# The S5 branch of a hybrid decoder trunk: recurrence per token, or per chunk of four tokens

## The reference

```python
uf = u.reshape(bsz, s, 32, 16)                   # 32 groups of 16 channels, 64 complex states each
ab = exp(lr * dt) * (cos(li * dt), sin(li * dt))  # one decay per group and state
bb = f * (b_re, b_im)                            # f from lambda and ab
x_re, x_im = einsum('bsgc,gpc->bsgp', uf, bb)     # inputs of the states
h[t] = ab * h[t - 1] + x[t]                      # complex, over all 256 tokens
y = einsum(h_re, c_re) - einsum(h_im, c_im) + d_skip * u
z = gelu(y); g = z @ w_glu + b_glu               # then a gated linear unit
```

## Time and profile before

| | us |
|---|---|
| median of 3 runs (858.77 to 859.50) | 858.96 |
| profiled execution | 857.93 |
| its span | 856.1 |
| mean granted clock of TensorE, share of full speed | 0.987 |
| TensorE busy | 825.7 |
| VectorE busy | 561.5 |
| ScalarE busy | 312.2 |
| POOL busy | 294.9 |

### The profile page before, as it was taken

How to read it: one execution, slowest core, us unless ns; L and a number is a source line. 1 busy time by engine, 2 the same in 40 slices (tenths; PEclk the granted TensorE clock), 3 DMA queues, 4 the chain that set the end, 5 groups by cost and what they waited for, 6 DMA issues and landing times.

```text
span 856.1 us, 10220 instructions
## 1 busy us (share of the span) xinstructions
PE 825.7 (96%) x3918; PEld 611.4 (71%) x3918; DVE 561.5 (66%) x939; ACT 312.2 (36%) x519; POOL 294.9 (34%) x130
## 2 busy tenths in 40 slices
...
GB/s 250 140 245 144 192 127 122 130 141 201 94 127 168 123 148 148 120 152 152 153 70 161 244 119 198 143 125 127 146 172 147 116 132 129 137 130 170 172 147 50
DMA packets 86992, 126.56 MB, mean 148 GB/s; under 512 B 22072, under 2 KB 32672, under 8 KB 86944
## 3 DMA queue, kind: packets, MB, share of 16 engines
...
...
q10 hardware_dynamic: 176, 0.04, 0.0%
HBM read 124.85 MB, written 1.05 MB: 147 GB/s over the span
## 4 chain that ended last, share of the span: by engine, by line
PE 59%; issue 29%; POOL 5%; DVE 3%; DMA 1%; ACT 1%; ACTq 0%; SPq 0%; POOLq 0%; DVEq 0%
PE proj L1480 29%; PE proj L1523 12%; PE proj L1519 6%; POOL w_lo L642 5%; PE M L1475 3%; PE M L1783 1%; PE M L1788 1%; DVE sc L1357 1%; PE M L1480 1%; DMA mt<-in_nsa_cv_w 1%; PE M L1753 1%; PE M L1807 1%; PE M L1806 1%; PE M L1624 1%; PE M L1805 1%
## 5 line engine op out<-in xcount | busy, mean ns | idle before, releaser
L642 POOL TENSOR_TENSOR w_lo<-raw,w_hi 128x1024 fp32r<-128x1024 f32 x112 | 286.3, 2586 | 504.9 <-ACT w_hi L660 473.9
L1523 PE MATMUL proj<-raw,h_full 128*128 128x512 f32 (+1 forms) x512 | 213.2, 572 | 0.0
L1523 PEld LDWEIGHTS proj<-raw,h_full 128*128 128x128 f32 x512 | 95.5, 190 | 104.7 <-issue 100.7
L660 ACT ACTIVATE w_hi<-raw 128x1024 fp32r<-128x1024 f32 x120 | 122.6, 1050 | 65.8 <-PE proj L1480 27.3
L1480 PE MATMUL proj<-w_hi,h_hi 128*128 128x512 f32 x320 | 128.4, 401 | 0.9 <-POOL w_lo L642 0.9
L1480 PE MATMUL proj<-w_lo,h_hi 128*128 128x512 f32 x320 | 124.9, 390 | 0.0
L1480 PE MATMUL proj<-w_hi,h_lo 128*128 128x512 f32 x320 | 124.8, 390 | 0.0
L1519 PE MATMUL proj<-h_full,raw 128*128 128x256 f32 x512 | 113.8, 381 | 0.0
L1519 PEld LDWEIGHTS proj<-h_full,raw 128*128 128x128 f32 x512 | 96.2, 190 | 14.1 <-issue 0.8
L1480 PEld LDWEIGHTS proj<-w_hi,h_hi 128*128 128x128 f32 x320 | 60.1, 188 | 14.4 <-issue 1.7
L1480 PEld LDWEIGHTS proj<-w_hi,h_lo 128*128 128x128 f32 x320 | 60.1, 188 | 13.0
...
## 6 DMA issues: line engine op xcount, KB each, us to landing
...
```

What stands on the lines that cost most here:

```text
L642: nc.gpsimd.tensor_tensor(w_lo[:, slot(s, l), 0:n * w], raw[:, u % N_RAW, 0:n * w], w_hi[:, slot(s, l), 0:n * w].bitcast(f32), ALU.subtrac ...
L660: i = nc.scalar.activation(out_, in_, func, **kw)
L1523: last = mm(ps[:, 512 * t:512 * t + w], h_full[:, k, t * P:(t + 1) * P], rw, start=st_, stop=sp_, skip_group_check=True)
```

## The change

S5 runs over 64 chunks of four tokens (LC = 4, NC5 = 64) instead of 256 tokens, in two halves h of eight pairs of groups (HS) instead of eight steps of two.

- Powers 1 to 4 of the decay are made on the chip in parameters_b. From them VectorE makes W (make_w: B times powers 0 to 3; 384 elements per operation) and V (make_v: C times powers 1 to 4; 512 elements); POOL zeroes two block-diagonal buffers, into which ScalarE spreads them (spread_w, spread_v: per half two copies of 64 partitions x 256, and four of 64 x 384 or 64 x 512).
- turn_w transposes W, 8 blocks of 128x128 in each of four calls, and keep_wT copies each of the four results (1024 elements) out. C is transposed as before; keep_v0 takes it over in four copies of 64 x 256. B is not transposed any more.
- keep_u brings u into a layout in which the four tokens of a chunk lie on four blocks of 32 partitions: 16 copies of 32 partitions x 256.
- state_inputs(h): 16 float32 products, 128x128 stationary, 64 columns. scan(h): the same operations as before on 512 elements, with two scans of 512 over eight sequences of 64 (a decay of zero stands at each start). state_outputs(h): for each pair two products of V with the states before the chunk, and one of a 128x128 block-lower matrix (ms) with the inputs, 24 products of 64 columns. That matrix comes from chunk_kernels(h), 16 products of 32 stationary columns with 128, in four column groups, and keep_ms, 16 copies of 32 partitions x 64 to 256. keep_y copies y back to the order of tokens, 16 copies of 32 x 128; skip adds the skip.
- ScalarE's split of h (h_hi) moves from behind the first trig to behind the evacuation of gate_s5. SyncE's load of ck waits for V instead of for turn_x. The scratch for dynamic DMA shrinks from 4096 to 2048.

```diff
+LC = 4
+NC5 = T // LC
+HS = NS5 // 2
...
-  bT_hi = sb("bT_hi", [P, 2, KB, P], f32r)
-  bT_lo = sb("bT_lo", [P, 2, KB, P], f32r)
-  cT = sb("cT", [P, 2, KB, P])
+  s5x = sb("s5x", [P, 4096])
+  powers = sb("powers", [P, 2, LC, NS5])
...
+  vk = cols(4096, 2560).rearrange("p (f s k g c) -> p f s k g c", f=2, s=HS, k=LC + 1, g=2)
...
+  c_nat = s5x[:, 0:1024].rearrange("p (f q g n) -> p f q g n", f=2, q=KB, g=2)
+  wT = s5x[:, 0:2048].rearrange("p (f s n) -> p f s n", f=2, s=HS)
+  ms = s5x[:, 2048:3072].rearrange("p (s n) -> p s n", s=HS)
+  s5_h = s5x[:, 3072:4096].rearrange("p (f s c) -> p f s c", f=2, s=HS)
+  wbd = gate[:, :, :, :].rearrange("p b k t -> p (b k t)").rearrange("p (f s e g c) -> p f s e g c", f=2, s=HS, e=LC, g=2)
...
         if name == "ck":
-            sp.wait_ge(xT_done, 4)
+            sp.wait_ge(v_ready, 2)
+            sp.wait_ge(vk_ready, 1)
...
+def zero_blocks(pool):
+    pool.memset(gate[:, :, :, :], 0.0)
+    pool.memset(cols(4096, 2560), 0.0).then_inc(blocks_zero, 1)
...
+    zero_blocks(pool)
+    pool.memset(s5x[:, 2048:4096], 0.0).then_inc(cleared, 1)
...
+if l + 1 < DEPTH:
+    gp.wait_ge(noT_done, 1)
+    gp.wait_ge(yg_lo, 4)
+    zero_blocks(pool)
...
+def trig(h):
+    act.wait_ge(ang_ready, h + 1)
+    if h:
+        act.wait_ge(h_done, h)
+    run(ang_r, ang_a, ACT.Abs, trig_done)
+    run(cos_sin[:, 1], ang_a, ACT.Sin, trig_done, scale=TURN)
+    act.wait_ge(trig_done, 3 * h + 2)
+    run(cos_sin[:, 0], ang_r, ACT.Sin, trig_done, scale=-TURN, bias=half_pi[:, 0:1])
+    run(ang_a[:, :, 1:NC5], bc(S(2)[:, HS * h:HS * h + HS].unsqueeze(2), [P, HS, NC5 - 1]), ACT.Copy)
+    run(ang_a[:, :, 0:1], S(2)[:, HS * h:HS * h + HS].unsqueeze(2), ACT.Copy, dec_ready, scale=0.0)
+def spread_w(h):
+    act.wait_ge(w_ready, h + 1)
+    if h:
+        act.wait_ge(kp_done, h)
+    else:
+        act.wait_ge(blocks_zero, 1)
+    for g in range(2):
+        r = slice(64 * g, 64 * g + 64)
+        run(wbd[r, :, :, 0, g, :], bb[r, :, HS * h:HS * h + HS, :], ACT.Copy)
+        for f in range(2):
+            run(wbd[r, f, :, 1:LC, g, :], w_sum[h][f][r].rearrange("p (s e c) -> p s e c", s=HS, e=LC - 1),
+                ACT.Copy, wbd_ready if f and g else None)
+def keep_wT(h, f):
+    act.wait_ge(wT_done, 2 * h + f + 1)
...
+def keep_v0():
+    act.wait_ge(cT_done, 1)
+    if l:
...
+def spread_v(h):
+    act.wait_ge(v_ready, h + 1)
+    if h:
+        act.wait_ge(y_done, h)
+    for g in range(2):
+        r = slice(64 * g, 64 * g + 64)
...
+def keep_u(e):
+    src = pr("u_s5")[:, :].rearrange("p (q c j) -> p q c j", q=KB, j=LC)[:, :, :, LC - 1 - e]
+    for d in range(4):
+        run(dst[32 * e:32 * e + 32, :, d, :], src[32 * d:32 * d + 32], ACT.Copy,
+            u_ready if e == LC - 1 and d == 3 else None)
+def keep_ms(h):
+    act.wait_ge(kp_done, h + 1)
+    if h:
+        act.wait_ge(y_done, h)
+    else:
+        scalar.wait_ge(cleared, 3)
+    for e in range(LC):
+        for d in range(4):
+            run(dst[32 * e:32 * e + 32, :, d, 32 * (LC - 1 - e):P], src[32 * d:32 * d + 32, :, 0:32 * (e + 1)],
+                ACT.Copy, ms_ready if e == LC - 1 and d == 3 else None)
+def keep_y(h):
+    act.wait_ge(y_done, h + 1)
+    for i in range(LC):
+        for d in range(4):
+            run(dst[32 * d:32 * d + 32, :, :, i], src[32 * i:32 * i + 32, :, d, :],
+                ACT.Copy, y_ready if i == LC - 1 and d == 3 else None)
+spread_w(0)
+trig(0)
+keep_v0()
+keep_wT(0, 0)
 next_cast("u_s5")
...
+keep_u(0)
+keep_u(1)
+keep_wT(0, 1)
+keep_u(2)
+keep_u(3)
+run(flat(u_s5[:, :, :]), pr("u_s5")[:, :], ACT.Copy, evac("u_s5"))
+spread_v(0)
...
+keep_ms(0)
+spread_w(1)
 next_cast("u_lru")
 run(u_lru[:, :, 3:T + 3], pr("u_lru")[:, :].rearrange("p (t n) -> p t n", t=KB), ACT.Copy, evac("u_lru"))
-trig(2)
+keep_wT(1, 0)
 next_cast("ret_v")
+act.wait_ge(wbd_ready, 2)
 run(flat(ret_v[:, :, :]), pr("ret_v")[:, :], ACT.Copy, evac("ret_v"))
+trig(1)
+keep_wT(1, 1)
+keep_y(0)
+spread_v(1)
+act.wait_ge(vk_ready, 2)
...
+keep_ms(1)
...
 gate_chunk("s5")
-trig(5)
+act.wait_ge(hfull_done, KD)
+for k in range(0, KD, 2):
+    run(flat(h_hi[:, k:k + 2, :]), flat(h_full[:, k:k + 2, :]), ACT.Copy, hhi_done)
+keep_y(1)
...
+    pw = [[powers[:, f, k, :] for k in range(LC)] for f in range(2)]
+    v.tensor_tensor(S(2), S(10), S(10), ALU.mult)
+    v.tensor_tensor(pw[1][0], S(15), S(10), ALU.mult)
+    link(v.tensor_tensor(pw[0][0], S(14), S(10), ALU.mult))
+    v.tensor_tensor(S(2), S(2), S(2), ALU.mult)
+    v.tensor_scalar(S(20), pw[0][0], 1.0, None, ALU.subtract)
+    for k, m in ((1, 0), (3, 1)):
+        v.tensor_tensor(S(26), pw[0][m], pw[0][m], ALU.mult)
+        v.scalar_tensor_tensor(pw[1][k], pw[0][m], 2.0, pw[1][m], ALU.mult, ALU.mult)
+        link(v.tensor_tensor(S(27), pw[1][m], pw[1][m], ALU.mult))
+        link(v.tensor_tensor(pw[0][k], S(26), S(27), ALU.subtract))
+    v.tensor_tensor(S(26), pw[0][1], pw[0][0], ALU.mult)
+    v.tensor_tensor(S(27), pw[1][1], pw[1][0], ALU.mult)
+    v.tensor_tensor(S(28), pw[0][1], pw[1][0], ALU.mult)
+    link(v.tensor_tensor(S(29), pw[1][1], pw[0][0], ALU.mult))
+    v.tensor_tensor(pw[0][2], S(26), S(27), ALU.subtract)
+    link(v.tensor_tensor(pw[1][2], S(28), S(29), ALU.add))
...
+def products(tmp, a0, a1, b0, b1, shape):
+    for n, (p, q) in enumerate(((a0, b0), (a1, b1), (a0, b1), (a1, b0))):
+        i = v.tensor_tensor(tmp[:, n].rearrange("p (s k c) -> p s k c", s=HS, c=16), p, q, ALU.mult)
     link(i)
+def make_w(h):
...
+    products(t, b0, b1, p0, p1, shape)
...
+def make_v(h):
...
+    products(t, c0, c1, p0, p1, shape)
...
+def angles(h):
+    shape = [P, HS, NC5]
+    if h:
+        dve.wait_ge(trig_done, 3 * h)
+        dve.wait_ge(dec_ready, h)
+    tm = bc(cst("time").rearrange("p (c j) -> p c j", j=LC)[:, :, 0].unsqueeze(1), shape)
+    hi, lo = (bc(S(i)[:, HS * h:HS * h + HS].unsqueeze(2), shape) for i in (16, 17))
+    v.tensor_tensor(ang_a, tm, hi, ALU.mult)
+    link(v.tensor_tensor(ang_b, tm, lo, ALU.mult))
+    link(v.tensor_tensor(ang_r, ang_a, ang_b, ALU.add))
+    link(v.tensor_scalar(ang_r, ang_r, ROUND, ROUND, ALU.add, ALU.subtract))
+    link(v.tensor_tensor(ang_a, ang_a, ang_r, ALU.subtract))
+    link(v.tensor_tensor(ang_a, ang_a, ang_b, ALU.add))
     v.tensor_scalar(ang_a, ang_a, 0.5, -0.5, ALU.min, ALU.max).then_inc(ang_ready, 1)
+def scan(h):
+    cos, sin = cos_sin[:, 0], cos_sin[:, 1]
     t0, t1, t2, t3 = (s5_t[:, f] for f in range(4))
...
+    dve.wait_ge(bu_done, h + 1)
     v.tensor_tensor(t0, re, cos, ALU.mult)
...
     v.tensor_tensor(t3, re, sin, ALU.mult).then_inc(bu_used, 1)
+    dve.wait_ge(bu_used, h + 1)
     v.tensor_tensor(t0, t0, t1, ALU.add)
     link(v.tensor_tensor(t2, t2, t3, ALU.subtract))
+    v.tensor_tensor_scan(flat(t1), flat(ang_a), flat(t0), 0.0, ALU.mult, ALU.add)
+    link(v.tensor_tensor_scan(flat(t3), flat(ang_a), flat(t2), 0.0, ALU.mult, ALU.add))
+    if h:
+        dve.wait_ge(y_done, h)
+    else:
+        vector.wait_ge(cleared, 3)
...
+    v.tensor_tensor(h_im, h_im, t2[:, :, n], ALU.add).then_inc(h_done, 1)
+dve.wait_ge(b_loaded, 32)
+for n, (f, b) in enumerate(((f_re, 0), (f_im, 1), (f_re, 1), (f_im, 0))):
+    i = v.tensor_tensor(b_tmp[:, n], b_nat[:, b], f, ALU.mult)
+link(i)
+v.tensor_tensor(bb[:, 0], b_tmp[:, 0], b_tmp[:, 1], ALU.subtract)
+link(v.tensor_tensor(bb[:, 1], b_tmp[:, 2], b_tmp[:, 3], ALU.add))
+make_w(0)
+angles(0)
+make_w(1)
...
+def skip(h):
+    dve.wait_ge(y_ready, h + 1)
+    for q in (2 * h, 2 * h + 1):
+        i = v.scalar_tensor_tensor(y_s5[:, q, :], u_s5[:, q, :], vec[:, V_D + q:V_D + q + 1], y_s5[:, q, :],
+                                   ALU.mult, ALU.add)
+    link(i)
...
+dve.wait_ge(v0_ready, 1)
+make_v(0)
+make_v(1)
...
+scan(0)
+angles(1)
+scan(1)
+skip(0)
...
+skip(1)
...
+def turn_c():
+    pe.wait_ge(hfull_done, KD)
+    pe.wait_ge(c_loaded, 64)
+    for f in range(2):
+        for q in range(KB):
+            last = tr(M[:, f, q * P:(q + 1) * P], c_nat[:, f, q].rearrange("p g n -> p (g n)"))
+    last.then_inc(cT_done, 1)
+def turn_w(h, f):
+    pe.wait_ge(wbd_ready, h + 1)
+    if h == 0 and f == 1:
+        pe.wait_ge(v0_ready, 1)
+    if h:
+        pe.wait_ge(bu_used, h)
+        pe.wait_ge(wT_ready, 2 * h + f)
+    bank = 0 if (h, f) == (0, 1) else 2
+    for s in range(HS):
+        last = tr(M[:, bank + s // 4, (s % 4) * P:(s % 4 + 1) * P], wbd[:, f, s].rearrange("p e g c -> p (e g c)"))
+    last.then_inc(wT_done, 1)
+def state_inputs(h):
+    pe.wait_ge(u_ready, 1)
+    pe.wait_ge(wT_ready, 2 * h + 2)
+    for s in range(HS):
         for f in range(2):
+            last = mm(M[:, 2 + f, s * NC5:(s + 1) * NC5], wT[:, f, s, :], uc[:, HS * h + s, :], start=True, stop=True)
     last.then_inc(bu_done, 1)
+def chunk_kernels(h):
+    pe.wait_ge(wT_ready, 2)
+    pe.wait_ge(vk_ready, h + 1)
+    pe.wait_ge(wbd_ready, h + 1)
+    if h:
+        pe.wait_ge(ms_ready, h)
+    for q in range(2):
         for f in range(2):
+            for d in range(4):
```

(59 more changed lines are left out.)

258 lines of the change are left out of this document (85 added, 173 removed).

## The result

The changed kernel takes 886.28 us (median of 4 runs, 883.74 to 886.77), the kernel before beside it 858.87: ratio 1.0316, interval 1.0297 to 1.0336, so 3.2% slower. The profiled execution took 886.77 us, its span 885.0, against 857.93 and 856.1 before. The forecast was 881, with a range of 868 to 890.

The account below looks back on a forecast made before the run. TensorE's work and its waits were taken to bound the kernel. From the profiled 857.9 us, 10.4 + 6.8 + 1.8 - 1.6 + 1.9 + 2.8 + 0.3 gave 880.3, as a median 881 us, range 868 to 890.

Parts of the forecast that it names:

- What bounds: Whole kernel: TensorE's work and its waits set the time; taking VectorE's scans away gives nothing by itself.
- Start: Start of the model, VectorE's diags beside POOL's memsets: no cost in the sum, 0 us.
- rival B: Layer 0 start: each diag waits for one POOL memset, x turned 2.5 us later, 1.8 of clock: 885; chance 0.2.
- its own last sentence: Forecast wrong if a 64-column product takes half its price, TensorE waits from u_lru to gate_s5, or first turn_x is late.
- Layer 0's chain: Up to state_inputs(0): TensorE waits 2.6 us before W's transposes and 2.3 for u; clock losses of 1.8 and 1.8.
- TensorE's work: S5 steps: 24.8 us added less 19.6 removed per layer, +5.2 each, +10.4 in all.
- cv and the middle: TensorE's wait at compress(1) for the load of cv goes, -1.6 us; no other wait from u_lru to gate_s5.
- Border: Between the layers, before turn_x: parameters_b adds 1.9 us, idle 3.75; clock loss +2.8.
- Layer 1: Start of layer 1: only keep_v0 to keep_u is exposed, +0.3 us.
- Elsewhere: Rest of the kernel: no cost in the sum, 0 us.

Follow-up runs that it names:

- the light scans: Kernel before with four of the six operations that turn the scanned states back left out in each of eight steps: 858.16 us, ratio 0.9997.
- the early memsets: Changed kernel with POOL's three memsets (gate, sc, s5x) moved ahead of its two inverse roots: 877.13 us, ratio 1.0233.
- later trig: Changed kernel with ScalarE's trig(0) of layer 0 moved behind the copy of u_s5: 875.36 us, ratio 1.0203.
- the half weights: Changed kernel with 64 stationary columns instead of 128 in all 160 products of state_inputs and state_outputs: 868.42 us (one run).
- the late parameters alone: Changed kernel with parameters_b of layer 1 moved behind the second diag: 885.67 us, ratio 1.0329.
- all three edits: Changed kernel with memsets before the inverse roots, trig(0) behind u_s5's copy, parameters_b(1) behind the second diag: 866.11 us (1.0094), again 866.52 (1.0093).

## Why the prediction held, and where it failed

**What bounds.** Right: TensorE's work and its waits are the time. 41 us less on VectorE in the kernel before bought nothing (the light scans, 0.9997), and the 140 us less in the changed kernel do not show as a gain anywhere.

**Start.** This step failed: the sum had nothing for it. The prediction named the collision as rival B and gave it 0.2, because a diag takes 0.24 us for 128 elements, no faster than a product, and so "hardly runs" in a two-port mode. At 128 elements most of the time is the start of the instruction, for 16 elements take 0.17; at 512 a tensor_scalar takes 0.43 us and a product 0.69 in the trace of before, and there the faster rate shows. B's price was off too: each diag was to wait for one memset, 2.5 us; in fact both wait for all three, and turn_x starts 5.25 later. B's 1.8 of clock was right (1.9 measured). The gain of the early memsets, 7.1, shows the cause. By its own last sentence, a late first turn_x was a sign that the forecast is wrong.

**Layer 0's chain.** Right in place and in order: waits in front of W's transposes and of state_inputs, and ScalarE's copies at 0.385. With the start out of the way (the early memsets) state_inputs(0) starts at 45.47, where 44.6 was forecast. The angles took 5.05 us instead of 4.0, because their two products (L1172, L1173) take 1.07 and 1.05 us for 512 elements and not the 0.69 of a plain one. Broadcast operands alone don't explain that, as make_v's products (L1139) have two of them as well and take 0.62 each, start to start; the angles' products also read the token numbers in steps of four, which no run varied. A third wait, in front of turn_w(0,1), was not seen, and the clock did not fall on cmp, where the forecast had it (two halves of 3.94 us), but behind the third wait. So there were 7.2 us of waiting for 5.0, and 5.0 of clock for 3.6. The clock's price was read from single waits. It is no fixed price either: after the same three waits it is 5.0 in the changed kernel and 3.3 with the early memsets. The later trig took away 5.2 of the 7.2 us of waiting and all of the clock.

**TensorE's work.** The price of 0.111 per record was right (5.30 us for 24 products, 3.57 for 16), and the half weights show why. The sum was too high, 10.4 against 5.8. chunk_kernels took 1.01 and 0.90 instead of 1.3. By rows the steps added in layer 0 take 24.3 us and those removed 19.7, so 4.6; measured were 3.2. The rest lies in the chunks, which the sum took as unchanged: the twelve half chunks of 512 columns from ret_v to ret_k take 84.17 us before, start to next start, and 82.55 in the changed kernel. A half with a step of the old S5 behind it takes 7.06 (60.72 to 67.78), one in the changed kernel that stands before turn_w 6.87.

**cv and the middle.** Right: the wait for cv is gone, and no wait shows from u_lru to gate_s5.

**Border.** The idle time of 3.75 was right (3.72). The clock, 2.8, was 1.6.

**Layer 1.** 0.50 for 0.3. Its slack was thin: the late parameters alone brought 1.17 us of waiting and over 3 of clock back there.

**Elsewhere.** 1.4 us lie behind ret_k, in pieces under 0.8, and their cause stays open. In the trace TensorE's wait for u_s is 4.1 us in the two layers instead of 0.9. That costs nothing: in both kernels and both layers the product behind this wait starts 7.77 or 7.78 us after the product that had waited 2.6 us for w_lo. So 3.2 of the 15.8 us of new idle time are no loss. The figure also differs between two runs of the same kernel, 1.0 and 4.1 with all three edits.

The sum for the profiled execution was 22.4 us and came out as 29.0. Too little were the start by 7.2, layer 0's waits by 2.2 and its clock by 1.4, and 1.6 in the rest; too much were the work by 4.6 and the border's clock by 1.2. That the time lies within the range is in part luck, for the step that failed at the start was offset by work that was priced too high. With rival B the forecast would have said 885, and with B's wait at its true length 888. In a better order of the same instructions 1.0094 of the kernel before is left, and that is the work.
